# The mixers' inverse roots on GpSimd: an addition and a power in place of a root and a reciprocal

## What is computed

```python
def layer_norm(x, g, b):
    mu = jnp.mean(xf, axis=-1, keepdims=True)
    var = jnp.mean(jnp.square(xf - mu), axis=-1, keepdims=True)
    y = (xf - mu) * lax.rsqrt(var + EPS)
...
    h = causal_depthwise_conv(h, dw_w, dw_b)
    h = layer_norm(h, ln_g, ln_b)
    return jax.nn.silu(h)
...
y = jnp.concatenate([rms_norm(y_nsa, g_nsa), rms_norm(y_gmlp, g_gmlp),
                     rms_norm(y_conv, g_conv)], axis=-1)
x = x + y @ w_out[l]
```

## Time and profile before

| | |
|---|---|
| median of 3 runs | 2496.66 us (2496.63 to 2497.34) |
| the profiled execution: its time | 2497.44 us |
| the profiled execution: its span | 2495.7 us |
| TensorE busy | 2481.7 us, 99% of the span |
| VectorE, ScalarE, GpSimd busy | 49%, 37%, 51% |
| granted TensorE clock, mean | 0.999 |
| attention stage, steps 4 to 15 | about 1870 to 1965 us of the span |

### The profile page before, as it was taken

The page is one execution under the profiler, slowest core; times in us unless marked ns, Lnnn a source line. Parts: engine busy times, 40 slices in busy tenths (PEclk is TensorE's granted clock), DMA queues, the critical chain, the costliest instruction groups (busy, mean ns, idle before and its releaser), DMA issues.

```text
span 2495.7 us, 34794 instructions
## 1 busy us (share of the span) xinstructions
PE 2481.7 (99%) x11916; PEld 2047.8 (82%) x11916; DVE 1225.0 (49%) x1439; ACT 919.1 (37%) x1332; POOL 1262.2 (51%) x882
## 2 busy tenths in 40 slices
PE   9999999999999999999999999999999999999998
PEld 7888888888888888888888888888877788888887
DVE  7444712453222542555125423227988855788363
ACT  5123533332222332335234322224367644444233
POOL 5555345555555544543455555555533443555455
PEclk9999999999999999999999999999999999999999
DMA  5332233333333333322333333336321232333332
GB/s 161 103 97 85 68 99 94 96 99 93 100 94 101 94 93 101 93 76 76 101 93 101 93 99 96 95 99 160 88 68 60 77 93 67 93 95 99 94 98 78
DMA packets 441997, 235.38 MB, mean 94 GB/s; under 512 B 16160, under 2 KB 436128, under 8 KB 441888
## 3 DMA queue, kind: packets, MB, share of 16 engines
q1 hardware_dynamic: 441456, 233.26, 32.4%
q10 hardware_dynamic: 432, 0.67, 0.1%
HBM read 231.81 MB, written 2.10 MB: 94 GB/s over the span
## 4 chain that ended last, share of the span: by engine, by line
PE 97%; DVE 1%; ACT 1%; issue 1%; POOL 0%; POOLq 0%; DVEq 0%; ACTq 0%
PE unit_ps L1880 62%; PE unit_ps L2032 13%; PE unit_ps L2018 8%; PE aux L1917 2%; PE unit_ps L2134 1%; PE aux L2160 1%; PE unit_ps L2128 1%; PE unit_ps L2201 1%; PE unit_ps L2404 1%; PE unit_ps L1917 1%; PE aux L2268 1%; PE o_banks L1917 1%; PE o_banks L1958 1%; PE aux L2316 1%; PE o_banks L2187 1%
## 5 line engine op out<-in xcount | busy, mean ns | idle before, releaser
L483 POOL TENSOR_TENSOR wl<-raw,wh 128x512 fp32r<-128x512 f32 x862 | 1252.8, 1474 | 1218.6 <-ACT wh L559 817.4
L559 ACT ACTIVATE wh<-raw 128x1024 fp32r<-128x1024 f32 x304 | 322.6, 1061 | 1032.4 <-PE unit_ps L1880 978.3
L1880 PE MATMUL unit_ps<-ah,wh 128*128 128x512 f32 x1280 | 501.7, 392 | 0.0
L1880 PE MATMUL unit_ps<-ah,wl 128*128 128x512 f32 x1280 | 498.6, 390 | 0.0
L1880 PE MATMUL unit_ps<-al,wh 128*128 128x512 f32 x1280 | 498.4, 389 | 0.0
L1880 PE MATMUL unit_ps<-bh,wh 128*128 128x512 f32 x768 | 300.0, 391 | 0.0
L1880 PE MATMUL unit_ps<-bh,wl 128*128 128x512 f32 x768 | 299.1, 389 | 0.0
L1880 PE MATMUL unit_ps<-bl,wh 128*128 128x512 f32 x768 | 299.1, 389 | 0.0
L1880 PEld LDWEIGHTS unit_ps<-ah,wl 128*128 128x128 f32 x1280 | 240.4, 188 | 50.1
L1880 PEld LDWEIGHTS unit_ps<-al,wh 128*128 128x128 f32 x1280 | 240.5, 188 | 49.8 <-issue 0.5
L1880 PEld LDWEIGHTS unit_ps<-ah,wh 128*128 128x128 f32 x1280 | 240.4, 188 | 49.7 <-issue 0.5
(11 more groups left out here) (417 smaller groups left out, 3867.8 us busy)
## 6 DMA issues: line engine op xcount, KB each, us to landing
raw<-w_in_dram SPq DMA_DIRECT2D x144, 512.0 KB, 4.0
raw<-w_up_dram SPq DMA_DIRECT2D x64, 512.0 KB, 4.0
raw<-w_down_dram SPq DMA_DIRECT2D x64, 512.0 KB, 4.1
raw<-up_dram SPq DMA_DIRECT2D x44, 512.0 KB, 3.8
raw<-w_conv_out_dram SPq DMA_DIRECT2D x16, 512.0 KB, 4.2
raw<-w_ret_out_dram SPq DMA_DIRECT2D x16, 512.0 KB, 4.2
raw<-w_o_dram SPq DMA_DIRECT2D x16, 512.0 KB, 4.1
raw<-down_dram SPq DMA_DIRECT2D x16, 512.0 KB, 3.8
```

Source lines behind the costliest of these rows:

```text
L483: last = pool.tensor_tensor(wl[j][:, half], raw[j % 2][:, half], wh[j][:, half].bitcast(F32), ALU.subtract)
L559: act.activation(wh[j][:], raw[j % 2][:], ACT.Copy).then_inc(w_hi, 1)
L1880: last = pe.matmul(unit_ps[j % 2][:], w[j][:, k], v[:, k * T:(k + 1) * T], start=(k == 0 and n == 0), stop=(k == KB - 1 and n == 2))
```

## The change

The three inverse roots move to GpSimd: it adds EPS to the tile (one `tensor_scalar`), waits for its own addition, and raises to the power -0.5 (one `tensor_tensor` with a column of -0.5 broadcast over the tile). GpSimd's loop over the units is opened up around the stage, so that these two instructions stand behind the units MK+8, MK+10 and MK+14. ScalarE's three roots and VectorE's three reciprocals go. VectorE waits for the results where it uses them: in step 7 ahead of the multiplications, in step 12 and in step 13 ahead of `part_norm`.

```diff
+MEAN_STEPS, ROOT_STEPS = (GM_STEP, CV_STEP, CV_STEP + 1, CV_STEP + 5), (GM_STEP, CV_STEP + 1, CV_STEP + 5)
...
+        root_arg, less_half = sem("root_arg"), sb("less_half", [P, 1])
...
+            pool.memset(less_half[:], -0.5)
...
-            units(pool, U_END // 4 * 4, body)
+            def inverse_root(n, t, s):
+                pool.wait_ge(mean_out, MEAN_STEPS.index(n) + 1)
+                pool.tensor_scalar(t, t, EPS, None, ALU.add).then_inc(root_arg, 1)
+                pool.wait_ge(root_arg, ROOT_STEPS.index(n) + 1)
+                pool.tensor_tensor(t, t, less_half[:].broadcast_to([P, T]), ALU.pow).then_inc(s, 1)
+
+            ROOTS = {GM_STEP: (part_r[1], part_std), CV_STEP + 1: (part_r[2], cv_std), CV_STEP + 5: (part_r[2], part_std)}
+            alone = MK // 4 * 4
+            units(pool, alone, body)
+            for u in range(alone, alone + 20):
+                body(u, u % 4)
+                if u - MK - 4 in ROOTS:
+                    inverse_root(u - MK - 4, *ROOTS[u - MK - 4])
+            units(pool, U_END // 4 * 4 - alone - 20, lambda u, j: body(u + (alone + 20), j))
...
-                if k == CV_STEP + 1:
-                    act.wait_ge(mean_out, 3)
-                    act.activation(part_r[2], part_r[2], ACT.Sqrt, bias=eps[:, 0:1]).then_inc(cv_std, 1)
-                    act.activation(part_r[1], part_r[1], ACT.Sqrt, bias=eps[:, 0:1]).then_inc(part_std, 1)
-                elif k == CV_STEP + 3:
+                if k == CV_STEP + 3:
...
-                elif k == CV_STEP + 5:
-                    act.wait_ge(mean_out, 4)
-                    act.activation(part_r[2], part_r[2], ACT.Sqrt, bias=eps[:, 0:1]).then_inc(part_std, 1)
...
                 elif k == CV_STEP + 2:
                     dve.wait_ge(cv_std, 1)
-                    go()
-                    did(dve.reciprocal(part_r[2], part_r[2]))
                     for i in range(2):
                         mult(y_cv[i], y_cv[i], part_r[2])
...
-                elif k == CV_STEP + 5:
-                    root_inverse(1, part_r[1])
-                elif k == CV_STEP + 6:
-                    root_inverse(2, part_r[2])
...
                 if k == GM_PARTS:
+                    dve.wait_ge(part_std, 1)
                     part_norm(0)
                     part_norm(1)
                 elif k == CV_PARTS:
                     part_lo(0)
                     part_lo(1)
+                    dve.wait_ge(part_std, 2)
                     part_norm(2)
                     part_norm(3)
```

More of the change, by code:

```diff
@@ L1528, in read_mean @@
                     copy(dst, unit_ps[0][:], mean_out)
-            def root_inverse(n, t):
-                dve.wait_ge(part_std, n)
-                go()
-                did(dve.reciprocal(t, t))
             def square_sum(s):
```

## The result

The changed kernel takes 2723.53 us in the median (2722.17 to 2724.44, 4 runs) against 2496.64 us before: 1.0908 times, 95% interval 1.0895 to 1.092, 226.9 us more. The prediction had said slower, but 2508 us and at most 2560.

What follows compares the result with a forecast made beforehand. TensorE, busy 2481.7 of 2495.7 us, was taken as the bound. Stops of 7.7 and 3.1 us less 0.6 gave 10.2 on 2496.7, plus 1 for the engines' return: 2508 us, range 2495.5 to 2560.

Steps and rivals of the forecast that it cites:

- What bounds the kernel, and what the change could give: Stage of the change: TensorE nearly always busy; removed roots and reciprocals gain at most its 0.6 us wait.
- what is removed was on the path: Rival: VectorE's 10 and ScalarE's 7 us of removed work held the kernel up; time near 2490 us; chance 0.02.
- The price of the power: GpSimd's power of 128x512 was taken as 13 us, between bounds of 1.25 and 28 us.
- the rival with the dear power: Rival: power over 28 us, stopping steps 9 and 13; 2553 us at 28, 2588 at 40; chance 0.15.
- Where it is waited for, and the sum: TensorE waits 7.7 us in step 9 and 3.1 in step 13, less 0.6: 10.2 us more.
- 2P - 18.3: Step 9 delay once two powers of duration P queue on GpSimd, holding from P = 12.6 us; 7.7 us at 13.
- P - 9.9: Step 13 cost of the third power, duration P, delaying the load of MK+17; 3.1 us at P = 13.
- The first place: VectorE in step 7 waits for the second power, delaying maxima and exponentials; TensorE stops 7.7 us in step 9.
- The slack of 5.7 us: First place: a power up to 5.7 us costs nothing, from 2.2 us of slack before TensorE's scores of step 10.
- nothing up to 10.6 us: Rival: a power under 10.6 us changes nothing that can be told; 2496 to 2501.5 us; chance 0.38.
- The second place: Step 13: the third power delays MK+15's low part, MK+17's load and ScalarE's split; TensorE stops 3.1 us.
- the return of three engines: 1 us added to the sum for three engines returning from the stop; TensorE's clock was left to the range.

Runs made afterwards that it cites:

- run with the multiplication: The changed kernel with each GpSimd power replaced by a multiplication with the same column of -0.5: 2495.51 us, 0.9995 times the kernel before.
- run with 32 columns: The changed kernel with the three powers on the first 32 of the 512 columns only: 2502.05 us, 1.0022 times the kernel before.

## Why the prediction was wrong

**What bounds the kernel, and what the change could give:** right. In the run with the multiplication TensorE's wait of 0.6 us is gone and the median is 1.1 us lower, above the 0.6 us that the prediction took for the gain and within the 1.3 us of TensorE's idle time that it named beside it. The rival "what is removed was on the path", near 2490 us, is out.

**The price of the power:** the step that failed. The prediction took 13 us, "each of the two functions as dear against GpSimd's plain instruction as the reciprocal is on VectorE", and as its upper bound the same factor twice, 28 us. It measured 82 us, 66 times the subtraction (1.25 us). The bound was no bound: nothing in the trace ties the price of one function on GpSimd to that of another function on VectorE. The text said so itself ("nothing in the trace bounds a function made in software") and still ended the range at 2560. An operation that the trace doesn't show in any form leaves the upper side open, and the rival with the dear power had to be given more than 0.15 and the range had to reach it. How GpSimd computes the power, and so why a column costs 0.159 us, stays open.

**Where it is waited for, and the sum:** the mechanism was right. With P = 81.95 the prediction's own terms give 2P - 18.3 = 145.6, P - 9.9 = 72.1, less 0.6: 217 us, and 222.1 us of added stops were measured. The engines, the units and the loads named for both places are those of the trace. Two details differ. The first place came in two stops, 63.6 and 86.3 us, since the load of MK+11 stopped TensorE ahead of VectorE's wait. The prediction gave that load no term because VectorE's wait would be the longer one, and this holds for the sum: the two stops are parts of one delay. Alone the first power is worth a stop of 63.1 us. And the stop was to come with the scores in step 9, but came with the turning in step 8.

**The slack of 5.7 us:** wrong, and it matters for the rival "nothing up to 10.6 us". At 5.45 us the cost is 5.2 us, at 10.56 us 13.7 us where 5 were said. Three terms were mis-sized. First, TensorE's first need behind the maxima is not the scores of step 10 (2.2 us of slack) but the copy queued behind the first exponential. The kernel before, ScalarE's row and then TensorE's:

```profile
1911.49 0.60 ACT L754 ACTIVATE c_f<-o_banks 128x512 f32<-128x512 f32 x1
...
1912.65 0.27 PE L2182 MATMUL o_banks<-ident,c_f 128*128 128x128 f32 x1
```

The copy ended at 1912.09 and TensorE used it at 1912.65, which leaves 0.6 us: 1.6 less than was counted. Second, the collision of VectorE's multiplications with GpSimd's subtraction costs 2.0 us. Third, from the start of the addition to the start of the power it is 1.6 us and not 1.2, twice 0.4 for two additions. By this count that is 4.4 us, whatever the power's duration once 2P - 18.3 is the term that holds, and the runs show it: with 128, 256 and 512 columns the first place has stops of 27.6, 68.3 and 149.9 us, where 2P - 18.3 gives 23.2, 64.0 and 145.6. The second place is right to within a us: 11.7, 31.9 and 72.8 us, where P - 9.9 gives 10.9, 31.3 and 72.1.

**The clock:** one us was added for "the return of three engines", and the fall of TensorE's clock was left to the range. The time grew by 4.8 us more than the stops (3.4 us by the profiled execution's own 2722.17 us). Windows of the changed kernel (stretch and its length, then busy us of PE, PEld, DVE, ACT and POOL, the granted clock, DMA share, GB/s), the first three ahead of, at the beginning and at the end of the first stop, the others around the end of the second:

```profile
1904.00:1914.00 10.00, 6.49 (x53) 4.71 (x51) 0.00 (x0) 2.02 (x7) 10.00 (x1) 1.00 0.01 2
1914.00:1924.00 10.00, 0.00 (x0) 0.00 (x0) 0.00 (x0) 0.00 (x0) 10.00 (x1) 0.54 0.00 0
1960.00:1970.00 10.00, 0.00 (x0) 0.00 (x0) 0.00 (x0) 0.00 (x0) 10.00 (x4) 0.50 0.00 0
...
2060.00:2065.00 5.00, 3.42 (x17) 3.07 (x19) 4.52 (x10) 4.21 (x14) 0.00 (x0) 0.51 0.17 58
2065.00:2070.00 5.00, 5.00 (x43) 3.50 (x40) 2.99 (x7) 2.71 (x7) 2.50 (x2) 1.00 0.10 18
```

The clock falls from 1.00 (2.4 GHz) to 0.50 (1.2 GHz) while TensorE stands still, and the first matmuls behind the stop run at 0.51; in the window behind, the clock is 1.00 again. A 128x256 matmul in the middle of a group takes up to 0.415 us there, for 0.283 in the median. The run with 32 columns shows what this costs behind one stop of 4.5 us:

```profile
1915.00:1920.00 5.00, 4.57 (x21) 3.73 (x23) 4.14 (x9) 4.69 (x14) 0.36 (x1) 0.51 0.00 0
```

The twelve matmuls of the unit's half that follow the stop take 2.84 us there (1915.56 to 1918.40) and 1.60 us before (1912.68 to 1914.28). These 1.2 us are most of the 1.3 us by which this run's time grew more than its stop. With the subtraction kept apart the stop was 2.5 us, the clock still went down, just behind it (0.66 over 1915 to 1920 us), and 1.1 us came on top. The runs with one root, each with one stop of 63 to 81 us, grew by 1.9 to 2.6 us more than their stops. So one stop costs between 1 and 2.6 us on top of its length, even one of 2.5 us; the three stops of the runs with 64 to 512 columns cost 2.7 to 5.6 us. The page "TensorE: Matmul & The Clock Gate" of the Trainium skill, which the prediction cited without a run to show it, has the fall to 1.2 GHz in its table of states (Part 1, "What's actually happening"); the trace agrees with 0.50. That the whole remainder of the longer stops is the clock's is argued from these rows; no run kept the clock up through a stop.

**The chances.** 0.15 was given to a power over 28 us, the case that came. "The power is cheap" had 0.38 up to a power of 10.6 us; the run with 32 columns costs 5.2 us, so the limit for 5 us lies at a power just under 5.45 us.

## What to carry to other kernels

An operation that no row of the trace shows has a lower bound and no upper one. Measure it by itself first, in the form and size that it will have: one run on scratch tiles gave the price here, and with it the prediction's own terms give the stops to within 6 us. Before moving work to an engine with idle time, ask what stands behind it in that engine's queue, and set its duration against the gap between two items there (GpSimd's gaps were 4.5 to 7.5 us), and not only against the distance to where its result is used. Both can bind: the queue did for the first and third roots, the result for the second. Slack is read at the first instruction behind the late one in each strict queue, the copy behind the exponential here, and not at the next one that uses the data.

## What the runs showed of the hardware

- GpSimd's power in fp32 takes 0.159 us for a column and 0.4 us fixed, whatever the number of partitions (1, 16 or 128: 20.70 to 20.72 us for 128 columns) and for exponents -0.5, 2 and 1.7 of the base 1.7. 128x512 takes 82 us, a multiplication 1.04 us.
- An addition of a constant to 128x512 fp32 takes 1.50 us on GpSimd, longer than the multiplication of two operands, one of them a broadcast column (1.04 us), or the subtraction that writes the low parts (1.25 us).
- VectorE's multiplication of two SBUF tiles of 128x512 goes from 0.71 to 1.72 us beside GpSimd's subtraction, and stays at 0.71 us beside its power. A wait that keeps multiplication and subtraction apart gave 2.0 us back to TensorE.
- TensorE's granted clock went from 1.00 to 0.50 in or just behind every stop of 2.5 us and more that was looked at, and the runs with one such stop took 1.1 to 2.6 us more than its length.
